# Queries and keys of two token mixers as four folded pairs with features on partitions

## The chip, the cores and the metric

The kernel runs on one core of a Trainium2 chip. The metric is the device time of one execution in microseconds (us). All arithmetic is in 32-bit floats. The engines are TensorE (PE, matmuls; its weight loads are shown apart as PEld), VectorE (DVE), ScalarE (ACT), GpSimd (POOL) and SyncE (SP, which issues nearly all transfers of weights).

## The reference

Two transformer blocks over 256 tokens of width 1024. The change lies in the first block's mixer, which runs two linear-attention branches (GLA with learned gates, retention with fixed decays) over the tokens ("latents") and takes its start states from 256 context tokens. Cut to what matters:

```python
def mixer_heads(h, w_in, gla_lr_w, gla_lr_b, gla_norm, states, rope):
    (gq, gk, gv, gg, glr_f, glr_b, rq, rk, rv, rg, m_gla, m_ret) = split_columns(h @ w_in)
    gq = heads(gq, GLA_HEADS) * GLA_DK ** -0.5          # 4 heads of 128
    gk, gv = heads(gk, GLA_HEADS), heads(gv, GLA_HEADS)
    def log_gate(lr, d):                                # lr: 16 columns a direction
        z = (lr @ gla_lr_w[d] + gla_lr_b[d]).astype(jnp.float32)
        return heads(jax.nn.log_sigmoid(z) / GLA_TAU, GLA_HEADS)
    o_f, s_gf = gla_scan(gq, gk, gv, log_gate(glr_f, 0), states[0], False)
    o_b, s_gb = gla_scan(flip(gq), flip(gk), flip(gv), flip(log_gate(glr_b, 1)), states[1], True)
    o_gla = rmsnorm(o_f + flip(o_b), gla_norm) * jax.nn.silu(heads(gg, GLA_HEADS))
    ...  # the same for retention with rq, rk, rv, rotated by axial_rope for the latents
```

It is computed once for the context (only the end states are used: keys and values) and once for the latents (queries, keys, values). gq, gk, rq, rk are 512 columns of `w_in` each. For the latents the kernel needs them with features on partitions and tokens on columns; for the context it needs the keys with tokens on partitions.

## The kernel before

**Stream and ring.** All large weights are a list of 1 MB column tiles (1024 x 256, laid out as 128 partitions x 2048). SP loads them in order into a ring of six; tile t is loaded once what read tile t - 6 is through (`FREED`, built by `plan()` beside `SUMS`, the order of all sums). `tile()` on PE waits for the landing of the next one. Besides the ring, SP loads eight tiles of another weight and the inputs at the start.

**Sums and banks.** `fresh(name)` takes PSUM banks 0 to 3 in turn and waits until the sum four places earlier was read (`sum_taken`). `feature_rows` computes one tile as 16 matmuls with weights stationary, 128 rows high, and 256 token columns moving (each matmul is two records in the trace).

**Folded pairs.** `folded` computes two column tiles (512 columns) of one or two sources as seven block products in place of eight. A block is 128 tokens x 512 of the inner dimension by 512 x 256 columns, 4 matmuls with activations stationary and 256 weight columns moving. Sources are the latents (banks 0 to 3, `hl`, `folds_l`, `parts_l`) and the context (banks 4 to 7, `hc`, `folds_c`, `parts_c`). The hand-overs are:

- DVE's `rows_fold` makes four sums of activation blocks (`rows_folded`), DVE's `weights_fold` changes the tiles in place in four steps (`weights_folded`); steps 1 and 2 wait for product 1, step 3 for product 2, step 4 for product 3.
- PE: product 2 waits for `rows_folded`, product 3 for ACT's first copy of a partial sum (`part_taken`), product 4 for its second copy and weight step 1, product 5 for step 3, product 6 for ACT's third copy, product 7 for step 4. Product 1 of the next pair waits until DVE's `blocks_summed` has made its third sum of this pair.
- ACT copies after products 1, 2 and 3; DVE sums blocks after products 4, 5, 6 and 7.

**Order around the change.** On PE, by hand: the 32 low-rank columns (`lr`); then for i = 0 to 3 two gate matmuls `z{i}0`, `z{i}1` (L1542) and one tile of `feature_rows` (L1366) out of gk0, gq0, gk1, gq1; the folded pair gkc (context only, on the two key tiles, which stay in the ring for it); folded pairs gv0, gv1 for both sources; four sums e (L1561, L1563) with the gates; rk0, rk1; rkc; rv0, rv1; rq0, rq1; eight state sums sg, sr (L1581); then the loop over eight heads with the gate tiles.

**The gates on ACT.** For each i: Abs and Relu of both z (L806, L808), Exp and Ln of both together (L810, L812), then the copy of the tile (L713). DVE adds the two parts (`la`, L2348). ACT begins block i when DVE has added block i - 1 (`la_ready`).

Of the kernel before, what the change touches and what calls it, by code (L numbers as in the profile page):

```python
# [7 lines left out]
ALU = mybir.AluOpType  # L8
# [141 lines left out]
def plan():  # L150
# [21 lines left out]
    for i, name in enumerate(("gk0", "gq0", "gk1", "gq1")):  # L172
        sums.extend([f"z{i}0", f"z{i}1"])
        tile(name)
        if name[1] == "k":
            freed[-1] = ("gkc.3",)
    folded("gkc")
    for p in range(2):
        folded(f"gv{p}")
        freed.extend([(f"gv{p}.3",)] * 2)  # L180
    sums.extend(f"e{d}{s}" for d in range(2) for s in range(2))
    for j in range(2):
        tile(f"rk{j}")
        freed[-1] = ("rkc.3",)
    folded("rkc")
    for p in range(2):
        folded(f"rv{p}")
        freed.extend([(f"rv{p}.3",)] * 2)
    for j in range(2):
        tile(f"rq{j}")  # L190
# [11 lines left out]

    def pair(name):

        folded(name)
        freed.extend([(f"{name}.3",)] * 2)
# [51 lines left out]
FOLDED_ROWS = {"gkc": 1, "gv0": 2, "gv1": 2, "rkc": 2, "rv0": 2, "rv1": 2, "mg0": 3, "mr0": 3, "mg1": 3, "mr1": 3,  # L258
# [9 lines left out]
def program(nc, stream, cdram, coldram, rowdram, biasdram, x, ctxt, cvec, wlr_d, wr_d, mem, wukv_d, out):  # L268
# [4 lines left out]
    with st:  # L273
# [217 lines left out]
        lr_ones, rows_zero = sem("lr_ones"), sem("rows_zero")  # L491
        la_ready, ctxk_ready = sem("la_ready"), sem("ctxk_ready")
# [53 lines left out]
        def turn_no(m):  # L546
            return m + (m >= 6) + (m >= 7)

# [151 lines left out]
        def _(act):  # L700
# [100 lines left out]
            for i in range(4):  # L801
                if i:
                    act.wait_ge(la_ready, 2 * i)
                for d in range(2):
                    b = take(f"z{i}{d}")
                    act.activation(spt[:, d, :], b[:, :], ACT.Abs).then_inc(act_step, 1)  # L806
                    act.wait_ge(act_step, step.one())
                    act.activation(la[:, i, d, :], b[:, :], ACT.Relu, scale=-1.0).then_inc(sum_taken, 1)  # L808
                    taken.one()
                act.activation(spt, spt, ACT.Exp, scale=-1.0).then_inc(act_step, 1)  # L810
                act.wait_ge(act_step, step.one())
                act.activation(spt, spt, ACT.Ln, bias=1.0).then_inc(act_step, 1)  # L812
                step.one()
                j = i // 2
                if i % 2 == 0:
                    copy(f"gk{j}", gk[:, 2 * j:2 * j + 2, :])
                else:
                    copy(f"gq{j}", gq[:, 2 * j:2 * j + 2, :], scale=DK ** -0.5)

            def folded(name, parts, firsts, between=None):  # L820

                at, part, _ = folded_at(name)
                act.wait_ge(sum_taken, at)
                for n in range(3):
                    if between and n:
                        between(n)
                    act.wait_ge(part_ready, part + n + 1)
                    for c, (p, first) in enumerate(zip(parts, firsts)):
                        b = bank[4 * c + (at + (2, 0, 2)[n]) % NB][:, 0:256]
                        ins = act.activation((p[:, 0, :], p[:, 1, :], first)[n], b, ACT.Copy)  # L830
                    ins.then_inc(part_taken, 1)
                for _ in range(4):
                    taken.one()

            folded("gkc", [parts_c], [gkc[:, 0, 0:256]])
# [9 lines left out]
            for j in range(2):  # L845
                copy(f"rk{j}", rqk[:, 2 * j:2 * j + 2, 1, :])
            folded("rkc", [parts_c], [rkc[:, 0, 0:256]])
# [3 lines left out]
            for j in range(2):  # L851
                copy(f"rq{j}", rqk[:, 2 * j:2 * j + 2, 0, :])
# [489 lines left out]
        def _(pe):  # L1342
# [36 lines left out]
            def folded(name, w0, w1, acts):  # L1379
# [6 lines left out]
                def product(slot, lhs, rhs, start):  # L1386
# [3 lines left out]
                    for c, source in enumerate(acts):  # L1390
                        b = bank[4 * c + (at + slot) % NB][:, 0:256]
                        for k in range(4):
                            mm = pe.matmul(b, lhs(*source, k), rhs[:, k, :], start=(start and k == 0), stop=(k == 3),  # L1393
                                           skip_group_check=True)
# [142 lines left out]
            key_tiles = []  # L1537
            for i in range(4):
                for d in range(2):
                    b = fresh(f"z{i}{d}")  # L1540
                    own = (wlr, wlr_own)[i // 2]
                    pe.matmul(b[:, :], lrT[0:65, 128 * (i % 2):128 * (i % 2) + 128], own[0:65, 512 * d:512 * d + 512],  # L1542
                              start=True, stop=True).then_inc(sum_ready, 1)
                w = tile()
                feature_rows(("gk0", "gq0", "gk1", "gq1")[i], w, hl)
                if i % 2 == 0:
                    key_tiles.append(w)
            latents, context = (hl, folds_l), (hc, folds_c)
            folded("gkc", *key_tiles, [context])
# [15 lines left out]
            key_tiles = []  # L1565
            for j in range(2):
                w = tile()
                feature_rows(f"rk{j}", w, hl)
                key_tiles.append(w)
            folded("rkc", *key_tiles, [context])  # L1570
            for p in range(2):
                folded(f"rv{p}", tile(), tile(), [latents, context])
            for j in range(2):
                feature_rows(f"rq{j}", tile(), hl)
# [617 lines left out]
        def _(dve):  # L2192
# [101 lines left out]

            def blocks_summed(name, parts, dsts, between=None):
# [15 lines left out]
                for c, (p, dst) in enumerate(zip(parts, dsts)):  # L2311
                    ins = dve.tensor_tensor(dst(0, 1), part_banks(at, c)[0], p[:, 2, :], ALU.add)
# [6 lines left out]
                for c, (p, dst) in enumerate(zip(parts, dsts)):  # L2319
                    ins = dve.tensor_tensor(dst(1, 1), p[:, 1, :], p[:, 0, :], ALU.add)  # L2320
# [5 lines left out]
                for c, (p, dst) in enumerate(zip(parts, dsts)):  # L2326
                    ins = dve.tensor_tensor(dst(1, 0), p[:, 0, :], part_banks(at, c)[3], ALU.subtract)
# [15 lines left out]
            rows_fold(hc, folds_c, ((0, 4),))  # L2343
            for n in range(8):
                i, d = divmod(n, 2)
                dve.wait_ge(sum_taken, NO[f"z{i}{d}"] + 1)
                dve.wait_ge(act_step, 4 * i + 4)
                dve.tensor_tensor(la[:, i, d, :], la[:, i, d, :], spt[:, n % 2, :], ALU.add).then_inc(la_ready, 1)  # L2348
                if n == 3:
                    rows_fold(hl, folds_l, ((0, 4),))  # L2350
            first = 5
            folded("gkc", [ring_tiles(first)[0], ring_tiles(first + 2)[0]], [parts_c], [block_of(gkc, 0)])
            for p in range(2):
                folded(f"gv{p}", ring_tiles(first + 4 + 2 * p), [parts_l, parts_c], [block_of(gv, 512 * p), block_of(gvc, 512 * p)])
# [5 lines left out]
            folded("rkc", ring_tiles(first + 8), [parts_c], [block_of(rkc, 0)])  # L2360
            dve.wait_ge(sum_taken, NO["rkc.3"] + 1)
# [7 lines left out]
            for p in range(2):  # L2369
                folded(f"rv{p}", ring_tiles(first + 10 + 2 * p), [parts_l, parts_c], [block_of(rv, 512 * p), block_of(rvc, 512 * p)])  # L2370
# [91 lines left out]
            dve.tensor_tensor(hvv[:, 0:4, :], mvv[:, 0:4, :, 0], mvv[:, 0:4, :, 0], ALU.mult).then_inc(dve_step, 1)  # L2462
            dve.wait_ge(dve_step, step.one())
            dve.tensor_tensor(hvv[:, 0:4, :], hvv[:, 0:4, :], mvv[:, 0:4, :, 1], ALU.add).then_inc(dve_step, 1)
# [844 lines left out]
```

## Time and profile before

| | |
|---|---|
| three timed runs, us | 1195.29, 1198.22, 1196.82 (median 1196.82) |
| the profiled execution: span, us (its own time goes from the first to the last instruction) | 1196.4 |
| PE busy | 1145.2 us, 96% |
| DVE busy | 493.8 us, 41% |
| ACT busy | 307.0 us, 26% |
| mean granted clock of TensorE | 0.987 of full speed |
| read from memory | 239.74 MB, mean 201 GB/s |

An engine's busy time is the union of its instructions' spans. Times in the trace count from the first instruction. The gap "idle before" of a row is the engine's idle time just before, with what released it. A share near 100% says which engine bounds the kernel over the whole; what an edit is worth is read in its own stretch.

### The profile page before, as it was taken

The page shows a single profiled execution, that of the slowest core. Times are in us where ns is not written, and L with a number is a line of the kernel's source. Part 1 is how long each engine was busy: PE and PEld are TensorE (multiplying, and loading weights), DVE is VectorE, ACT ScalarE, POOL GpSimd, SP SyncE. Part 2 cuts the span into 40 slices and gives each one's busy share as a digit, 9 for nine tenths or more (in the row PEclk, how much of TensorE's full clock was granted, in tenths as well). Part 3 has the DMA queues.
Part 4 walks back from the last instruction along what each step waited for, and adds up shares of the span by engine and source line. Part 5 has one row for each costly group of instructions (what it writes and reads, how often), then busy time and mean ns, then how long its engine had stood idle before and what let it go on. Part 6 is the DMA issues. An engine that isn't in the chain of part 4 may idle for free.

```text
span 1196.4 us, 15887 instructions
## 1 busy us (share of the span) xinstructions
PE 1145.2 (96%) x6452; PEld 844.0 (71%) x6452; DVE 493.8 (41%) x1114; ACT 307.0 (26%) x714; POOL 25.4 (2%) x43
## 2 busy tenths in 40 slices
PE   7999999999999999989999999889888989999998
PEld 6688888888877888865555554467656858887443
DVE  2324334304535676342222222328876432225555
ACT  4381010035213311141111110243484231000000
POOL 0000000000000030000000000010000000000000
PEclk9999999999999999999999999999889999999999
DMA  9933112322388445548999999623300414444540
GB/s 381 389 149 141 71 71 80 134 74 101 136 327 335 188 148 234 215 159 339 425 427 424 426 425 425 275 106 127 121 1 18 187 46 155 160 141 168 174 150 35
DMA packets 34727, 241.85 MB, mean 202 GB/s; under 512 B 3946, under 2 KB 4202, under 8 KB 6364
## 3 DMA queue, kind: packets, MB, share of 16 engines
q1 hardware_dynamic: 33500, 234.46, 49.7%
q0 software_dynamic: 720, 3.12, 0.7%
q10 hardware_dynamic: 432, 3.23, 0.6%
q8 instruction: 53, 0.87, 0.3%
q14 instruction: 22, 0.18, 0.0%
HBM read 239.74 MB, written 1.05 MB: 201 GB/s over the span
## 4 chain that ended last, share of the span: by engine, by line
PE 89%; DVE 3%; ACT 3%; DMA 2%; SPq 1%; issue 1%; DVEq 0%; ACTq 0%
PE bank L1393 20%; PE bank L1366 13%; PE bank L1783 9%; PE bank L1375 9%; PE bank L2139 8%; PE bank L1810 5%; PE bank L1441 4%; PE bank L1745 3%; PE bank L1752 2%; DMA arena<-in_stream 2%; PE bank L1461 1%; PE bank L1633 1%; PE bank L1636 1%; PE bank L1581 1%; PE bank L2118 1%; SPq L581 1%
## 5 line engine op out<-in xcount | busy, mean ns | idle before, releaser
L1393 PE MATMUL bank<-ring,arena 128*128 128x256 f32 x784 | 173.5, 380 | 0.7 <-ACT arena L1225 0.7
L1393 PEld LDWEIGHTS bank<-ring,arena 128*128 128x128 f32 x784 | 149.1, 190 | 21.1 <-ACT arena L1225 1.0
L1366 PE MATMUL bank<-arena,ring 128*128 128x256 f32 x480 | 103.8, 380 | 0.0
L1366 PEld LDWEIGHTS bank<-arena,ring 128*128 128x128 f32 x480 | 91.4, 190 | 12.2
L713 ACT ACTIVATE arena<-bank 128x512 f32<-128x512 f32 x58 | 34.1, 601 | 202.8 <-PE bank L1366 136.2
L1375 PE MATMUL bank<-ring,arena 128*128 128x256 f32 x320 | 71.1, 381 | 0.0
L1375 PEld LDWEIGHTS bank<-ring,arena 128*128 128x128 f32 x320 | 60.6, 191 | 9.1 <-issue 0.8
L1783 PE MATMUL bank<-ring,arena 128*64 128x256 f32 x512 | 57.0, 381 | 0.0
L830 ACT ACTIVATE arena<-bank 128x256 f32<-128x256 f32 x60 | 21.7, 382 | 136.9 <-PE bank L1393 136.9
L1375 PE MATMUL bank<-ring,hTl 128*128 128x256 f32 x256 | 56.6, 380 | 0.0
L1366 PE MATMUL bank<-hTl,ring 128*128 128x256 f32 x256 | 56.2, 380 | 0.0
L1366 PEld LDWEIGHTS bank<-hTl,ring 128*128 128x128 f32 x256 | 48.8, 190 | 8.6 <-issue 2.4
L1375 PEld LDWEIGHTS bank<-ring,hTl 128*128 128x128 f32 x256 | 48.4, 190 | 8.0 <-issue 1.9
L1783 PEld LDWEIGHTS bank<-ring,arena 128*64 128x64 f32 x512 | 36.0, 137 | 24.0 <-issue 6.7
L1441 PE MATMUL bank<-ring,arena 128*128 128x256 f32 x224 | 51.4, 386 | 1.7 <-ACT arena L713 0.8
L1441 PEld LDWEIGHTS bank<-ring,arena 128*128 128x128 f32 x224 | 42.6, 194 | 8.3 <-ACT arena L713 1.0
L1048 ACT ACTIVATE arena<-bank 128x256 f32<-128x256 f32 x16 | 6.1, 383 | 157.9 <-PE bank L1783 157.9
L1393 PE MATMUL bank<-ring,hTl 128*128 128x256 f32 x192 | 45.6, 381 | 0.4 <-ACT arena L713 0.4
L2694 DVE TENSOR_TENSOR arena<-arena,bank 128x256 f32<-128x256 f32 x16 | 6.7, 422 | 94.5 <-ACT arena L1048 94.5
L3159 DVE TENSOR_TENSOR arena<-arena 128x512 f32<-128x512 f32 x16 | 11.1, 692 | 75.7 <-ACT arena L713 75.7
L1393 PEld LDWEIGHTS bank<-ring,hTl 128*128 128x128 f32 x192 | 36.3, 190 | 5.8 <-issue 1.1
L2700 DVE TENSOR_TENSOR consts<-bank,arena 64x512 f32<-64x512 f32 x32 | 22.0, 688 | 38.6 <-PE bank L1810 38.4
(506 smaller groups left out, 1772.7 us busy)
## 6 DMA issues: line engine op xcount, KB each, us to landing
ring<-in_stream SPq DMA_DIRECT2D x163, 1024.0 KB, 7.0
arena<-in_stream SPq DMA_DIRECT2D x38, 1024.0 KB, 13.5
hTl<-in_stream SPq DMA_DIRECT2D x9, 1024.0 KB, 11.4
hTc<-in_stream SPq DMA_DIRECT2D x9, 1024.0 KB, 13.3
consts<-in_consts ACTq DMA_DIRECT2D x1, 3081.0 KB, 17.2
arena<-in_mem SPq DMA_DIRECT2D x2, 512.0 KB, 4.7
arena<-in_x SPq DMA_DIRECT2D x1, 1024.0 KB, 18.7
arena<-in_ctx SPq DMA_DIRECT2D x1, 1024.0 KB, 23.2
```

The costliest lines, as they stand in the source:

```text
L713: act.activation(dst, b[:, :].rearrange("p (a b) -> p a b", b=two), func, scale=scale).then_inc(sum_taken, 1)
L830: ins = act.activation((p[:, 0, :], p[:, 1, :], first)[n], b, ACT.Copy)
L1366: mm = pe.matmul(b[:, 256 * n:256 * n + 256], w[:, k, 128 * n:128 * n + 128], h[:, k, :], start=(k == 0), stop=(k == KD - 1))
L1375: mm = pe.matmul(b[:, 256 * i:256 * i + 256], h[:, k, 128 * i:128 * i + 128], w[:, k, :], start=(k == 0), stop=(k == KD - 1))
L1393: mm = pe.matmul(b, lhs(*source, k), rhs[:, k, :], start=(start and k == 0), stop=(k == 3), skip_group_check=True)
L1441: mm = pe.matmul(b[:, 256 * i:256 * i + 256], h[:, k, 128 * i:128 * i + 128], w[:, k, :], start=(k == 0 and i == 0), stop=(k == KD - 1), s ...
L1745: mm = pe.matmul(bank[1 + k % 2][:, 256 * j:256 * j + 256], xn2[:, j, 128 * k:128 * k + 128], Pm[:, j, :], start=True, stop=True)
L1752: mm = pe.matmul(acc[2 * j + n][:, :], hT_PT[j][:, 256:384], expert_rows(j, quad)[:, 512 * n:512 * n + 512], start=False, stop=False, skip ...
L1783: mm = pe.matmul(bank[0][CAP * e:CAP * e + CAP, FF * a:FF * a + FF], rows_k[:, at:at + CAP], w[e][:, k, :], start=(k == 0), stop=(k == KD ...
L1810: mm = pe.matmul(bank[1 + m][to:to + CT, :], hT_PT[n % 2][:, of:of + CT], wd[e][:, k, 512 * m:512 * m + 512], start=(k == 0), stop=(k == 1 ...
L2139: mm = pe.matmul(prod[m][:, :], lhs, rhs, start=(q == 0), stop=(q == 15))
L2700: ins = dve.tensor_tensor(expert_rows(g ^ n % 2, n // 2)[own, c], bank[1 + m][own, :], g2bc[own, c], ALU.mult)
```

## The change

1. gq, rq, gk and rk of the latents are computed as four folded pairs of column tiles. For features on partitions the roles in a matmul are exchanged: the (folded) weights are stationary, 128 columns at a time, and 128 tokens of the (folded) activations move. A product is then 8 matmuls of 128 columns. gk and rk take the context along as second source, in the old form.
2. The order becomes: z00, z01, z10, z11, gq, z20, z21, z30, z31, rq, gk with context, gv0, gv1, e, rk with context, rv0, rv1, states. The stream of tiles is put in the same order.
3. The gate matmuls go to banks 4 to 7 with semaphores of their own (`z_ready`, `z_taken`). ACT runs gates 0 before gq's copies, Abs and Relu of gates 1 between gq's second and third copy, Exp and Ln after the third; the same with gates 2 and 3 around rq.
4. DVE folds the rows of the latents first; its order is: gates 0, weight folds of gq, gates 1, row folds of the context, sums of gq, gates 2, weight folds of rq, gates 3, sums of rq, then gk.
5. The scale of gq by 128 ** -0.5 falls away, and the eps of the GLA head norm is multiplied by 128 instead; one small DVE operation is saved there.

```diff
             def folded(name, w0, w1, acts, features=False):
...
                         for k in range(4):
+                            if features and c == 0:
+                                for n in range(2):
+                                    mm = pe.matmul(b[:, 128 * n:128 * n + 128], rhs[:, k, 128 * n:128 * n + 128], lhs(*source, k),
+                                                   start=(start and k == 0 and n == 0), stop=(k == 3), skip_group_check=True)
+                            else:
+                                mm = pe.matmul(b, lhs(*source, k), rhs[:, k, :], start=(start and k == 0), stop=(k == 3),
+                                               skip_group_check=True)
...
...
@@ PE
-            key_tiles = []
+            latents, context = (hl, folds_l), (hc, folds_c)
             for i in range(4):
                 for d in range(2):
-                    b = fresh(f"z{i}{d}")
                     own = (wlr, wlr_own)[i // 2]
+                    if i >= 2:
+                        pe.wait_ge(z_taken, 2 * i + d - 3)
+                    pe.matmul(bank[4 + (2 * i + d) % 4][:, :], lrT[0:65, 128 * (i % 2):128 * (i % 2) + 128],
+                              own[0:65, 512 * d:512 * d + 512], start=True, stop=True).then_inc(z_ready, 1)
-                w = tile()
-                feature_rows(("gk0", "gq0", "gk1", "gq1")[i], w, hl)
...
-            folded("gkc", *key_tiles, [context])
+                if i % 2 == 1:
+                    folded(("gq", "rq")[i // 2], tile(), tile(), [latents], features=True)
+            pe.wait_ge(z_taken, 8)
+            folded("gk", tile(), tile(), [latents, context], features=True)
...
-            folded("rkc", *key_tiles, [context])
+            folded("rk", tile(), tile(), [latents, context], features=True)
...
-            for j in range(2):
-                feature_rows(f"rq{j}", tile(), hl)
@@ ACT
+            for i, (name, first) in enumerate((("gq", head_block(gq)(0, 0)), ("rq", head_block(rqk[:, :, 0, :])(0, 0)))):
+                gates_begun(2 * i)
+                gates_ended()
+                folded(name, [parts_l], [first], between_gates(2 * i + 1))
+                gates_ended()
+            folded("gk", [parts_l, parts_c], [head_block(gk)(0, 0), gkc[:, 0, 0:256]])
@@ DVE
-            rows_fold(hc, folds_c, ((0, 4),))
...
+            rows_fold(hl, folds_l, ((0, 4),))
...
+            for i, (name, v) in enumerate((("gq", gq), ("rq", rqk[:, :, 0, :]))):
+                gates_added(2 * i)
+                weights_fold(name, *ring_tiles(first + 2 * i))
+                gates_added(2 * i + 1)
+                if i == 0:
+                    rows_fold(hc, folds_c, ((0, 4),))
+                blocks_summed(name, [parts_l], [head_block(v)])
```

## Rows read from the trace of the kernel before

**Rows 1.** The page: busy time, DMA share in 40 slices, chain by engine.

```profile
PE 1145.2 (96%) x6452; PEld 844.0 (71%) x6452; DVE 493.8 (41%) x1114; ACT 307.0 (26%) x714; POOL 25.4 (2%) x43
...
DMA  9933112322388445548999999623300414444540
...
PE 89%; DVE 3%; ACT 3%; DMA 2%; SPq 1%; issue 1%; DVEq 0%; ACTq 0%
```

**Rows 2.** PE timeline, 56 to 92 us: start, length, engine, line, operation, tiles, count.

```profile
56.65 1.96 PE L1542 MATMUL bank<-arena 65*128 65x512 f32 x4 [0.68 <-ACT arena L799]
...
67.07 7.07 PE L1366 MATMUL bank<-hTl,ring 128*128 128x256 f32 x32
...
91.23 1.03 PE L1393 MATMUL bank<-ring,hTc 128*128 128x256 f32 x4
```

**Rows 3.** Windows: length, busy time and count by engine, granted clock, DMA share, GB/s.

```profile
91.23:103.32 12.09, 12.09 (x57) 10.66 (x56) 7.91 (x11) 1.75 (x4) 0.00 (x0) 1.00 0.00 1
103.32:127.50 24.18, 24.18 (x114) 21.33 (x113) 9.02 (x15) 1.98 (x6) 0.00 (x0) 1.00 0.43 174
156.82:170.63 13.81, 13.81 (x65) 12.19 (x64) 1.34 (x3) 1.19 (x2) 0.00 (x0) 1.00 0.12 51
```

**Rows 4.** PE timeline at 293 us; loads by line: count, busy, mean ns.

```profile
293.43 0.39 PE L1608 MATMUL bank<-arena 128*128 128x128 f32 x2
...
294.55 0.39 PE L1613 MATMUL bank<-arena 128*128 128x128 f32 x2
...
L1393 PEld LDWEIGHTS bank<-ring,arena 128*128 128x128 f32 x784 | 149.1, 190 | 21.1 <-ACT arena L1225 1.0 <-DVE arena L2265 0.4
```

**Rows 5.** ACT timeline, 57.5 to 94 us.

```profile
57.79 0.60 ACT L806 ACTIVATE arena<-bank 128x512 f32<-128x512 f32 x1 [1.39 <-PE bank L1542]
...
60.15 1.28 ACT L810 ACT_TABLE_LOAD   x1
...
63.81 1.06 ACT L812 ACTIVATE arena<-arena 128x1024 f32<-128x1024 f32 x1
...
93.22 0.38 ACT L830 ACTIVATE arena<-bank 128x256 f32<-128x256 f32 x1 [1.19 <-PE bank L1393]
```

**Rows 6.** DVE timeline, 64 to 100 us and 407.4 to 410.4 us.

```profile
64.97 1.29 DVE L2348 TENSOR_TENSOR arena<-arena 128x512 f32<-128x512 f32 x2 [8.69 <-ACT arena L812]
...
74.87 0.68 DVE L2262 TENSOR_TENSOR arena<-hTl 128x512 f32<-128x512 f32 x1
...
76.92 0.69 DVE L2265 TENSOR_TENSOR arena<-hTl,arena 128x512 f32<-128x512 f32 x1
...
93.16 1.23 DVE L2273 TENSOR_TENSOR ring<-ring 128x1024 f32<-128x1024 f32 x1 [0.96 <-PE bank L1393]
...
96.96 1.23 DVE L2280 TENSOR_TENSOR ring<-ring 128x1024 f32<-128x1024 f32 x1
...
407.46 0.42 DVE L2303 TENSOR_TENSOR arena<-bank,arena 128x256 f32<-128x256 f32 x1
...
409.11 0.43 DVE L2320 TENSOR_TENSOR arena<-arena 128x256 f32<-128x256 f32 x1
```

**Rows 7.** The ring's load issued at 28.5 us: its duration and time to landing.

```profile
L568 SPq DMA_DIRECT2D ring<-in_stream x1: 439/439/439, 28.5 to 28.5; - x1
...
DMA to landing us min/median/max: 33.8/33.8/33.8
```

**Rows 8.** PE timeline at 375 us.

```profile
375.77 0.48 PE L1393 MATMUL bank<-ring,hTl 128*128 128x256 f32 x1
```

**Rows 9.** Windows at pauses of PE and behind them, columns as in rows 3.

```profile
846.10:848.20 2.10, 0.07 (x1) 0.07 (x2) 2.07 (x5) 1.69 (x4) 0.00 (x0) 1.00 0.72 289
848.40:855.20 6.80, 6.11 (x31) 4.52 (x30) 5.09 (x28) 4.32 (x13) 0.00 (x0) 0.50 0.11 45
763.80:765.40 1.60, 0.09 (x5) 0.03 (x1) 1.38 (x2) 0.00 (x0) 0.00 (x0) 1.00 1.11 440
765.40:769.00 3.60, 3.60 (x8) 1.42 (x8) 0.00 (x0) 0.00 (x0) 0.00 (x0) 1.00 0.91 325
```

More of the change, by code:

```diff
@@ L170, in folded, with pair @@
         sums.extend(f"{name}.{n}" for n in range(4))
[L172 to L180, printed above, removed]
-    sums.extend(f"e{d}{s}" for d in range(2) for s in range(2))
-    for j in range(2):
[L183 to L190, printed above, removed]
+    def pair(name):
+        folded(name)
+        freed.extend([(f"{name}.3",)] * 2)
+    for name in ("gq", "rq", "gk", "gv0", "gv1"):
+        pair(name)
+    sums.extend(f"e{d}{s}" for d in range(2) for s in range(2))
+    for name in ("rk", "rv0", "rv1"):
+        pair(name)
     sums.extend(f"sg{h}" for h in range(HEADS))
@@ L800, in _ @@
             taken.one()
[L801 to L818, printed above, removed]
             def folded(name, parts, firsts, between=None):
@@ L829, in folded @@
                         b = bank[4 * c + (at + (2, 0, 2)[n]) % NB][:, 0:256]
+                        if n == 2 and len(first.shape) == 3:
+                            b = halves(b)
                         ins = act.activation((p[:, 0, :], p[:, 1, :], first)[n], b, ACT.Copy)
@@ L833, in folded, with gates_begun, gates_ended, between_gates @@
                     taken.one()
-            folded("gkc", [parts_c], [gkc[:, 0, 0:256]])
+            def gates_begun(i):
+                if i:
+                    act.wait_ge(la_ready, 2 * i)
+                for d in range(2):
+                    act.wait_ge(z_ready, 2 * i + d + 1)
+                    b = bank[4 + (2 * i + d) % 4]
+                    act.activation(spt[:, d, :], b[:, :], ACT.Abs).then_inc(act_step, 1)
+                    act.wait_ge(act_step, step.one())
+                    act.activation(la[:, i, d, :], b[:, :], ACT.Relu, scale=-1.0).then_inc(z_taken, 1)
+            def gates_ended():
+                act.activation(spt, spt, ACT.Exp, scale=-1.0).then_inc(act_step, 1)
+                act.wait_ge(act_step, step.one())
+                act.activation(spt, spt, ACT.Ln, bias=1.0).then_inc(act_step, 1)
+                step.one()
+            def between_gates(i):
+                def run(n):
+                    if n == 2:
+                        gates_begun(i)
+                return run
+            for i, (name, first) in enumerate((("gq", head_block(gq)(0, 0)), ("rq", head_block(rqk[:, :, 0, :])(0, 0)))):
[4 more added lines that the diff above has]
+            folded("gk", [parts_l, parts_c], [head_block(gk)(0, 0), gkc[:, 0, 0:256]])
             for p in range(2):
@@ L844, in _ @@
                     taken.one()
-            for j in range(2):
-                copy(f"rk{j}", rqk[:, 2 * j:2 * j + 2, 1, :])
-            folded("rkc", [parts_c], [rkc[:, 0, 0:256]])
+            folded("rk", [parts_l, parts_c], [head_block(rqk[:, :, 1, :])(0, 0), rkc[:, 0, 0:256]])
             for p in range(2):
@@ L2369, in _ @@
             for p in range(2):
[L2370 removed]
+                folded(f"rv{p}", ring_tiles(first + 12 + 2 * p), [parts_l, parts_c], [block_of(rv, 512 * p), block_of(rvc, 512 * p)])
             def gla_factors(h):
```

75 lines of the change are left out of this document (30 added, 45 removed).

## The prediction

> **What bounds the kernel now.** I read the page first: PE's busy line, the DMA slices and the chain [rows 1]. TensorE (PE) is busy 96% of the span and makes 89% of the chain that ended last. The other engines lie far below. So a shorter sum of PE work shortens the kernel, as long as nothing opens a gap on PE. Next I read PE's timeline of the changed stretch [rows 2] and its windows [rows 3]. From 56.65 us PE runs without a pause: two gate matmuls, then one column tile, four times over; a tile is half of the 13.81 us of [rows 3], 6.91 us, and 8.63 us is what one round takes ((91.23 - 56.65) / 4 = 8.64), so the two gate matmuls take 1.72. At 91.23 the first folded pair starts. The windows of the products are full to the last hundredth, at a granted clock of 1.00. The reader is to see that this stretch has no slack on PE and, so far, no gap either.
>
> Then I asked what the other engines do there, because the change reorders exactly their hand-overs. ScalarE (ACT) works 7.1 us on each block of gates: from 57.79 to 60.15 the four Abs and Relu, to 64.87 Exp and Ln, each behind a table load of 1.28 us [rows 5]. VectorE (DVE) waits for ACT and adds two halves in 1.29 us [rows 6]. Each block of ACT lies beside 8.63 us of PE work (1.72 + 6.91), and only one small copy per block ties PE to ACT. That is why it is hidden. The ring's loads are late as well: the DMA engines are full in the first two slices, to 60 us [rows 1].
>
> **The change part by part: PE's work.** Four pairs (gq, rq, gk, rk) are eight tiles of 6.91 us, 55.3 us by [rows 3] (13.81 for two). In their place stand 4 x 7 products of 8 matmuls that are 128 wide. The nearest rows are the six score matmuls of a head [rows 4]: each is two records, and five of them start within 1.12 us, from 293.43 to 294.55, so 0.223 each. A product takes 8 x 0.223 = 1.78 us, a pair 12.49, four pairs 50.0: 5.3 us less. Half the width does not cost exactly half (0.432 for 256 columns, since 6.91 us hold 16), for each record still loads 128 weight columns. Its load is on record with 190 ns [rows 4], and two of them are in flight at a time. The bounds of this price: 0.216, half of 0.432, gives 1.6 us less over 224 matmuls; a load that could not overlap the next one gives 0.380 a matmul, 35 us more. I take 0.223, as these rows are of the same width and type.
>
> The Trainium skill, "TensorE: Matmul & The Clock Gate", Part 3 (what overlaps and what doesn't), says that a weight load overlaps matmuls in flight only where its row group differs. All loads here have full height, so by this rule the four pairs would cost load and stream in turn, and the change would lose heavily. The trace disagrees: full-height matmuls follow each other at 0.223 us although two loads of 190 ns belong to each.
>
> The context halves of gk and rk (7 products of 4 matmuls, 12.09 us for each pair [rows 3]) stay as they are, inside the same pair. The eight gate matmuls stay too, 0.86 us each. New for DVE are four weight folds of 1.23 us for each of gq and rq, and for all four pairs the sums of the latents, 0.42 us an operation [rows 6]; ACT copies three blocks of 0.38 us a pair in place of two tiles [rows 5]. For gk and rk this lies beside 24.6 us of PE: in the two-sided value pair, with the same folds, copies and sums, DVE is busy 9.02 us of 24.18 and PE has no gap [rows 3]. For gq and rq, beside 12.5 us of PE, it must be followed hand-over by hand-over.
>
> **Where the early stretch gets its gaps.** Three things move, and on PE all later work is queued behind each wait. (a) gq now needs both its tiles before its first matmul. The second of them, tile 6, is issued at 28.5 us and lands after 33.8 us, at 62.3 [rows 7]; before, it was needed only at 67.07. PE's four gate matmuls end at 56.65 + 4 x 0.86 = 60.1, and everything on PE is queued behind the wait until 62.35: **first gap 2.25 us**. Nothing in the change alters the loads queued ahead of it. (b) PE's third and fourth products wait for ACT copies, which stand behind a whole block of gates; the fifth waits for the third weight fold, which DVE starts after adding that block. Block 0 ends on ACT at 64.87, DVE adds until 66.2, and the four folds take 5.03 us from 93.16 to 98.19 in the rows, with waits between them, so they are done at about +1.2, +2.4, +3.7 and +5.0 [rows 6]: 67.4, 68.6, 69.9, 71.2. Products one to three run 62.35 to 67.7, the fourth to 69.5, the fifth starts at 70.0, and gq ends at 70.0 + 3 x 1.78 = 75.35. (c) The sums of gq stand on DVE behind block 1 and the context fold. ACT starts block 1 after the second copy and after DVE has added block 0 (66.3), so 66.5 to 68.85, copies the first block of gq until 69.25 and ends block 1 at 74.0. DVE adds to 75.3, folds the context rows in 2.7 us to 78.0 and reaches the third sum 2.1 us later (407.46 to 409.54 in the rows), 80.1 [rows 6]. PE has done four gate matmuls to 78.8 and cannot start rq before 80.15: **second gap 1.35 us**.
>
> rq repeats it. Block 2 starts 1.14 us after its first gate matmul (57.79 against 56.65 in [rows 2, 5]), which is at 75.35, so 76.5 to 83.55. PE's third product waits for its copy (84.0), DVE adds to 84.9 and folds at 86.1, 87.3, 88.6, 89.9. The fourth product starts at 86.2, the fifth at 88.7, the pair ends at 94.05. ACT's block 3: 85.0 to 87.35, copy to 87.75, end 92.5; DVE adds to 93.8, and sums to 95.9. gk starts at 96.0: **third gap 1.95 us**. Before, the pair with the context keys starts at 91.23 [rows 2]. So this stretch, with the same four tiles, ends 4.8 us later.
>
> **What is given back.** From there on all is on PE, as in the two-sided value pairs, which have no gap [rows 3]. gk and rk cost 7 x (1.78 + 1.73) = 24.56 us each, 49.1 together. Removed are 12.09 + 13.81 + 12.09 + 13.81 = 51.8. That is 2.7 us less. The state products follow rv1 directly instead of rq; they need its banks one at a time, the last 5.2 us after the pair, and DVE's last sum takes under 1 us. SP's queue: the ring tile of the fifth gate is now released by rv1's last product instead of 6.9 us earlier, and is used only after eight state products and four gate tiles, over 40 us later. The DVE edit of the head variances removes one operation on 8 columns; PE is in the adaptive rows' matmuls meanwhile and starts its next pair at 375.77 with no idle time [rows 8], so it is worth nothing. Without that cover it would be worth at most what four such operations take, under 1 us. The removed scale of gq costs nothing either way.
>
> Sum at full clock: +4.8 - 2.7 = **+2.1 us**.
>
> **The clock.** The rows behind an idle PE are the part that tips it [rows 9]. After 2.1 idle us at 846.1 the granted clock was 0.50 for 6.8 us; two more pauses of 1.9 and 2.4 us, from 958.6 and 796.7, were followed by 0.50 as well; after a pause of 1.5 us at 763.8 it stayed 1.00. 0.50 is the lower of the engine's two levels, 1.2 GHz. The first and third gap are like those that a fall followed. The shortest falls in the trace last 3.4 us, the one of the rows 6.8, and I take 3.4: it costs 1.7 us of PE work. After the first gap 0.5 of it hides in the wait for the third weight fold, and 1.2 remain: gq ends at 76.55, all later chains follow, and the second gap becomes about 2.05. After the third gap it costs all 1.7, as gk has no slack. Sum: 2.1 + 1.2 + 1.7 = +5.0 us. The profiled execution has 1196.4 us of span, 0.4 under the median of the runs shown, so the forecast on the runs' side is 1196.8 + 5.0 = 1201.8 us.
>
> **Rivals.** (1) Gaps without falls of the clock: +2.1, 1198.9 us. For it: the stretch is at 1.00 today; against it: [rows 9]. (2) Also the second gap is followed by a fall: it delays rq's third product and so block 3, about +1.7, 1203.6 us. (3) The other side: DVE and ACT keep up, so that only PE's sum counts. The mechanism is the hand-over before gk: with gk's start at 93.9 the change is worth nothing, before 91.5 it is over 0.2% faster, and with no gap at all 5.3 us, 1191.5. Against it: ACT's four blocks and the copies between them (4 x 7.08 + 6 x 0.38) lead from 57.8 to 88.4 without any wait, with DVE's add and sums to 91.9, so a gk start before 91.5 asks for ACT blocks shorter than the rows show. (4) The new matmuls do not hold 0.223 in long runs, but wait for each load of 190 ns in turn: +35 us, 1232. The row group rule of the Trainium skill above is this case; the rows of scores speak against it.
>
> **How the numbers follow.** What a measurement of this kernel can tell from no change is about 0.2%, 2.4 us. My forecast with its falls has 0.5, rival 2 0.19, rival 1 0.24, rival 3 0.05, rival 4 0.02. Rival 1 lies at +2.1, just within 0.2%, and I leave 0.04 of it above. So slower is 0.5 + 0.19 + 0.02 + 0.04 = 0.75, within 0.2% is the other 0.20 of rival 1, and faster 0.05. The range reaches from rival 1 with part of the cheaper bound of the width, 0.5 of 1.6 us (1198.4), to rival 2 with 0.8 us for waits of DVE or ACT that last a little longer than read (1204.4).
>
> **What would show it.** In the changed trace: PE idle from about 60 to 62.3 in front of its first 128-wide matmul with the ring's DMA as releaser; gq's end near 75 to 77; idle 1 to 2 us before rq and about 2 before gk, both released by DVE; gk's start at 96 to 99; a granted clock of 0.5 in one or two short windows between 63 and 102 us; 0.223 us a matmul elsewhere; everything after rv1 merely shifted. The prediction is wrong if tile 6 lands early, if DVE's sums reach their third stage before PE is through its gate matmuls, or if the clock stays at 1.00.

## The result and the profile after

The changed kernel takes 1202.94 us (median of 14 runs, 1196.65 to 1206.99) against 1196.12 us for the kernel before (14 runs). The ratio is 1.0051, with a 95% interval of 1.0039 to 1.0063: 6.1 us slower, between 4.7 and 7.5. The prediction said 1201.8 us, 5.0 us slower. The profiled execution has a span of 1200.8 us, 4.4 us over that of before.

The page of the changed kernel, its busy line, the granted clock in slices and the chain by engine, against [rows 1]:

```profile
PE 1139.2 (95%) x6644; PEld 842.1 (70%) x6644; DVE 512.0 (43%) x1145; ACT 305.7 (25%) x718; POOL 25.5 (2%) x43
...
PEclk9999999999999999999999999989999999999999
...
PE 86%; ACT 5%; DVE 4%; DMA 2%; SPq 1%; issue 1%; DVEq 0%; ACTq 0%
```

PE is busy 6.0 us less than before, and the kernel is slower all the same. (Not all of the 6.0 us is work saved: the mean granted clock of the two executions differs too, 0.990 after and 0.987 before.) So PE has more idle time, and its share of the chain fell from 89% to 86% in favour of ACT (3% to 5%) and DVE (3% to 4%).

PE's timeline of the changed stretch, against [rows 2] (start, length, engine, line, operation, count, and idle time before with what ended it; L1399 are the 128-wide matmuls, L1402 the others of a folded pair):

```profile
57.92 3.67 PE L1552 MATMUL bank<-arena 65*128 65x512 f32 x8 [0.57 <-ACT arena L793]
63.75 2.96 PE L1399 MATMUL bank<-hTl,ring 128*128 128x128 f32 x16 [2.16 <-issue]
...
77.96 3.60 PE L1552 MATMUL bank<-arena 65*128 65x512 f32 x8
83.46 2.02 PE L1399 MATMUL bank<-hTl,ring 128*128 128x128 f32 x16 [1.90 <-DVE arena L2327]
85.32 1.95 PE L1399 MATMUL bank<-arena,ring 128*128 128x128 f32 x16
87.11 1.95 PE L1399 MATMUL bank<-hTl,ring 128*128 128x128 f32 x16
88.89 1.97 PE L1399 MATMUL bank<-arena,ring 128*128 128x128 f32 x16
91.21 3.84 PE L1399 MATMUL bank<-arena,ring 128*128 128x128 f32 x32 [0.35 <-DVE ring L2278]
...
98.47 2.02 PE L1399 MATMUL bank<-hTl,ring 128*128 128x128 f32 x16 [1.64 <-DVE arena L2327]
100.33 1.89 PE L1402 MATMUL bank<-ring,hTc 128*128 128x256 f32 x8
```

The reader is to see three gaps: 2.16 us before gq, 1.90 before rq, 1.64 before gk, and 0.35 inside rq. (The idle time of a row counts from the recorded end of the matmul before. Counted from where the next matmul would have started, which is how the prediction counts, the three are 2.39, 2.06 and 1.79 us.) Within rq the products start 1.79 us apart (85.32, 87.11, 88.89), so the new matmuls take 0.223 us each (1.79 / 8). From the first gate matmul to the first product of gk PE needs 98.47 - 57.92 = 40.55 us; before it needed 91.23 - 56.65 = 34.58 for its gates and four tiles. That is 6.0 us more.

The load of tile 6, against [rows 7], and windows as in [rows 3], one behind the first gap and one over the pair gk:

```profile
L562 SPq DMA_DIRECT2D ring<-in_stream x1: 430/430/430, 29.0 to 29.0; - x1
...
DMA to landing us min/median/max: 34.6/34.6/34.6
```

```profile
65.10:68.50 3.40, 3.40 (x20) 3.40 (x20) 2.26 (x3) 1.42 (x2) 0.00 (x0) 0.57 1.02 419
98.47:123.14 24.67, 24.66 (x168) 23.23 (x169) 8.78 (x15) 1.98 (x6) 0.00 (x0) 1.00 0.20 83
```

Tile 6 lands at 29.0 + 34.6 = 63.6, and gq starts at 63.75. The granted clock is 0.57 in the window from 65.1, the lower level in nearly all of it, after PE stood for 2.16 us. The pair gk is full: 24.67 us, against 24.56 forecast.

ACT and DVE in the same stretch, against [rows 5] and [rows 6]:

```profile
65.08 1.06 ACT L827 ACTIVATE arena<-arena 128x1024 f32<-128x1024 f32 x1
...
75.81 1.06 ACT L827 ACTIVATE arena<-arena 128x1024 f32<-128x1024 f32 x1
79.08 0.60 ACT L819 ACTIVATE arena<-bank 128x512 f32<-128x512 f32 x1 [2.22 <-PE bank L1552]
...
87.59 0.60 ACT L819 ACTIVATE arena<-bank 128x512 f32<-128x512 f32 x1
...
93.89 1.06 ACT L827 ACTIVATE arena<-arena 128x1024 f32<-128x1024 f32 x1
```

```profile
66.24 1.29 DVE L2358 TENSOR_TENSOR arena<-arena 128x512 f32<-128x512 f32 x2 [8.58 <-ACT arena L827]
...
76.96 1.29 DVE L2358 TENSOR_TENSOR arena<-arena 128x512 f32<-128x512 f32 x2 [4.50 <-ACT arena L827]
78.17 0.68 DVE L2263 TENSOR_TENSOR arena<-hTc 128x512 f32<-128x512 f32 x1
...
82.89 0.42 DVE L2327 TENSOR_TENSOR arena<-arena 128x256 f32<-128x256 f32 x1 [0.53 <-DVE arena L2322]
...
95.05 1.29 DVE L2358 TENSOR_TENSOR arena<-arena 128x512 f32<-128x512 f32 x2 [2.57 <-ACT arena L827]
...
97.90 0.42 DVE L2327 TENSOR_TENSOR arena<-arena 128x256 f32<-128x256 f32 x1
```

Ln of block 0 ends at 66.14 and DVE adds from 66.24. Ln of block 1 ends at 76.87; DVE adds from 76.96, folds the context from 78.17, and makes its third sum (L2327) from 82.89; rq starts at 83.46. Ln of block 3 ends at 94.95; DVE adds from 95.05 and makes the third sum from 97.90; gk starts at 98.47. Block 2 could begin only at 79.08, behind its gate matmuls. Both gaps stand behind ACT's gate blocks.

The balance of the profiled execution: +6.0 to the start of gk, and +1.3 that lie ahead of the change, where the first gate matmul comes at 57.92 instead of 56.65. In six of the kernels profiled below it comes at 56.5 to 56.8, so this part belongs to one execution. From the start of gk to the first state product PE needs 151.11 us (98.47 to 249.58), and before it needed 153.65 from its first pair on (91.23 to 244.88): 2.5 us less. So the state products start 4.7 us later than before, and the whole execution ends 4.4 us later.

### The profile page after: what moved, and what is told of

It is laid out like the page before. It is cut to its first block, busy times and chain, and to the rows that moved or that the text cites. A ratio compares the mean times of both kernels' runs of the same rounds, so it can differ in the third digit from the quotient of the medians.

```text
span 1200.8 us, 16320 instructions
## 1 busy us (share of the span) xinstructions
PE 1139.2 (95%) x6644; PEld 842.1 (70%) x6644; DVE 512.0 (43%) x1145; ACT 305.7 (25%) x718; POOL 25.5 (2%) x43
## 4 chain that ended last, share of the span: by engine, by line
PE 86%; ACT 5%; DVE 4%; DMA 2%; SPq 1%; issue 1%; DVEq 0%; ACTq 0%
PE bank L1402 20%; PE bank L1784 9%; PE bank L1370 9%; PE bank L1379 8%; PE bank L2140 8%; PE bank L1811 5%; PE bank L1450 4%; PE bank L1399 3%; PE bank L1746 3%; PE bank L1753 2%; DMA arena<-in_stream 2%; PE bank L1470 1%; PE bank L1634 1%; PE bank L1637 1%; PE bank L1582 1%
## 5 line engine op out<-in xcount | busy, mean ns | idle before, releaser
L1402 PE MATMUL bank<-ring,arena 128*128 128x256 f32 x784 | 174.2, 379 | 1.0 <-ACT arena L1229 0.7
L1402 PEld LDWEIGHTS bank<-ring,arena 128*128 128x128 f32 x784 | 148.1, 190 | 21.3 <-ACT arena L1229 1.0
L707 ACT ACTIVATE arena<-bank 128x512 f32<-128x512 f32 x50 | 29.4, 602 | 176.8 <-PE bank L1370 94.6
L807 ACT ACTIVATE arena<-bank 128x256 f32<-128x256 f32 x72 | 25.6, 382 | 168.5 <-PE bank L1402 165.0
L1379 PEld LDWEIGHTS bank<-ring,arena 128*128 128x128 f32 x320 | 60.3, 190 | 10.4 <-DMA ring<-in_stream 1.6
L1052 ACT ACTIVATE arena<-bank 128x256 f32<-128x256 f32 x16 | 6.1, 384 | 157.9 <-PE bank L1784 157.9
L1402 PE MATMUL bank<-ring,hTl 128*128 128x256 f32 x192 | 45.6, 380 | 0.3 <-ACT arena L707 0.3
L1402 PEld LDWEIGHTS bank<-ring,hTl 128*128 128x128 f32 x192 | 36.2, 190 | 5.8 <-issue 1.0
L2715 DVE TENSOR_TENSOR arena<-bank,arena 64x512 f32<-64x512 f32 x32 | 22.0, 689 | 38.6 <-PE bank L1811 38.3
L1746 PE MATMUL bank<-arena 128*128 128x256 f32 x128 | 35.5, 408 | 1.9 <-DVE arena L2675 1.9
```

The costliest lines, as they stand in the source:

```text
L707: act.activation(dst, b[:, :].rearrange("p (a b) -> p a b", b=two), func, scale=scale).then_inc(sum_taken, 1)
L1379: mm = pe.matmul(b[:, 256 * i:256 * i + 256], h[:, k, 128 * i:128 * i + 128], w[:, k, :], start=(k == 0), stop=(k == KD - 1))
L1746: mm = pe.matmul(bank[1 + k % 2][:, 256 * j:256 * j + 256], xn2[:, j, 128 * k:128 * k + 128], Pm[:, j, :], start=True, stop=True)
L2715: ins = dve.tensor_tensor(expert_rows(g ^ n % 2, n // 2)[own, c], bank[1 + m][own, :], g2bc[own, c], ALU.mult)
```

## The experiments

Theory A is that of the prediction: the new matmuls save their 1.33 us a pair, and the loss is made by the hand-overs around the gates, with falls of the clock behind the gaps. Theory B: the exchanged roles themselves cost the time. All ratios are to the kernel before, from runs beside it. The timeline of each kernel is that of one execution.

**Only rk and rq folded, behind the gates.** The kernel before, with these parts of the change alone:

```diff
-            for j in range(2):
-                w = tile()
-                feature_rows(f"rk{j}", w, hl)
-                key_tiles.append(w)
-            folded("rkc", *key_tiles, [context])
+            folded("rk", tile(), tile(), [latents, context], features=True)
             for p in range(2):
                 folded(f"rv{p}", tile(), tile(), [latents, context])
-            for j in range(2):
-                feature_rows(f"rq{j}", tile(), hl)
+            folded("rq", tile(), tile(), [latents], features=True)
```

> The kernel before, with only rk (with the context) and rq folded with features on partitions, both behind the gates, rq still behind rv1. Theory A (the loss is made by the hand-overs to ScalarE and VectorE around the gates; the new matmuls cost 0.223 us each): no idle time of TensorE in these pairs, each 1.33 us shorter than its two tiles, 2.7 us in all, so about 1193.5 us against 1196.2, ratio 0.998. Theory B (the exchanged roles cost time: 128-wide matmuls or their weight loads run slower in long runs than the six score matmuls): half of the loss of the changed kernel, ratio 1.002 or more, products of more than 1.9 us.

Measured: 1194.01 us, ratio 0.9985 (0.9972 to 0.9997), 1.8 us faster; the expected 0.998 lies inside. PE's timeline of rq in this kernel:

```profile
233.49 1.95 PE L1399 MATMUL bank<-hTl,ring 128*128 128x128 f32 x16
235.28 1.95 PE L1399 MATMUL bank<-arena,ring 128*128 128x128 f32 x16
...
246.00 1.25 PE L1584 MATMUL bank<-arena 128*128 128x256 f32 x5
```

rq takes 246.00 - 233.49 = 12.51 us, against 13.81 for its two tiles [rows 3], and from 150 to 262 us no row of PE shows idle time before it. Theory B falls: half of the change, placed elsewhere, is a gain. The first rows of this kernel show something else, which concerns the kernel before too:

```profile
56.74 1.96 PE L1551 MATMUL bank<-arena 65*128 65x512 f32 x4 [0.68 <-ACT arena L804]
60.39 8.86 PE L1370 MATMUL bank<-hTl,ring 128*128 128x256 f32 x32 [1.70 <-DMA ring<-in_stream]
```

Its first tile landed at 60.3 us in this execution (issued at 28.7, 31.6 to landing) where it landed at 57.5 before (28.1 and 29.4). PE stood for 1.70 us, and the group of this tile's matmuls lasts 8.86 us where it is 7.07 in [rows 2]: from 61.4 to 63.1 the granted clock is 0.50. The first pair starts at 94.97, 38.23 us after the first gate matmul, where it is 34.58 in [rows 2]. So this execution loses 3.65 us in the old order, in code that the edit does not touch, and its span of 1196.5 us is the longest of the 12.

**The context fold moved to the start.**

```diff
             rows_fold(hl, folds_l, ((0, 4),))
+            rows_fold(hc, folds_c, ((0, 4),))
...
                 gates_added(2 * i + 1)
-                if i == 0:
-                    rows_fold(hc, folds_c, ((0, 4),))
                 blocks_summed(name, [parts_l], [head_block(v)])
```

> The changed kernel, with VectorE's fold of the context rows (2.7 us) moved from ahead of the sums of gq to the idle time before the gates. Theory A1 (ScalarE's gate blocks carry the chain): the gap before rq closes, but rq's third product then waits for the copy behind gate block 2 for about 1.7 us, gk starts where it did within 0.3 us, ratio to the kernel before stays at 1.004 to 1.006 (a little less where one fall of the clock fewer follows). Theory A2 (VectorE's queue carries it): gk starts 1.5 to 2 us earlier, ratio 1.003.

Measured: 1199.86 us, ratio 1.0037 (1.0018 to 1.0055). PE's timeline:

```profile
56.64 3.67 PE L1552 MATMUL bank<-arena 65*128 65x512 f32 x8 [0.57 <-ACT arena L793]
...
80.14 1.95 PE L1399 MATMUL bank<-hTl,ring 128*128 128x128 f32 x16
81.93 1.95 PE L1399 MATMUL bank<-arena,ring 128*128 128x128 f32 x16
85.23 2.05 PE L1399 MATMUL bank<-hTl,ring 128*128 128x128 f32 x16 [1.35 <-ACT arena L807]
87.58 2.02 PE L1399 MATMUL bank<-arena,ring 128*128 128x128 f32 x16 [0.30 <-DVE ring L2274]
...
97.22 2.02 PE L1399 MATMUL bank<-hTl,ring 128*128 128x128 f32 x16 [1.64 <-DVE arena L2327]
```

And the first operation of gate block 3 on ACT:

```profile
86.34 0.60 ACT L819 ACTIVATE arena<-bank 128x512 f32<-128x512 f32 x1 [0.88 <-DVE arena L2359]
```

rq starts without a gap, and then its third product waits 1.35 us for ACT's copy, the fourth 0.30 and the fifth 0.35 us for weight folds. gk starts 97.22 - 56.64 = 40.58 us after the first gate matmul, where the changed kernel has 40.55. The loss was moved, not removed: theory A1. The reason is on ACT: block 3 waits for DVE's addition of block 2, and begins 29.70 us after the first gate matmul (86.34 - 56.64), where it begins after 29.67 in the changed kernel (87.59 - 57.92). So closing the second gap brings gk no nearer. The ratio is lower than 1.0051, with overlapping intervals; fewer falls of the clock would explain it, but this run does not settle that.

**The sums of rq ahead of adding gates 3.**

```diff
-                gates_added(2 * i + 1)
                 if i == 0:
+                    gates_added(1)
                     rows_fold(hc, folds_c, ((0, 4),))
                 blocks_summed(name, [parts_l], [head_block(v)])
+                if i == 1:
+                    gates_added(3)
```

> The changed kernel, with VectorE's sums of rq ahead of its addition of gate block 3. Theory A: the third gap (1.64 us before gk) closes, gk starts 1.6 us earlier, and a fall of the clock behind it becomes rarer: 2 to 3 us less than the changed kernel, ratio to the kernel before about 1.003. Theory B (cost in the matmuls): no change to the changed kernel, 1.005.

Measured: 1198.55 us, ratio 1.0012 (0.9995 to 1.0029), so 4.7 us less than the changed kernel by the ratios, more than the 2 to 3 that were expected; why it is more stays open. PE's timeline, and windows behind its first two gaps:

```profile
56.66 3.67 PE L1552 MATMUL bank<-arena 65*128 65x512 f32 x8 [0.57 <-ACT arena L793]
...
81.89 3.13 PE L1399 MATMUL bank<-hTl,ring 128*128 128x128 f32 x16 [1.90 <-DVE arena L2327]
...
94.31 3.74 PE L1399 MATMUL bank<-hTl,ring 128*128 128x128 f32 x32
```

```profile
62.10:65.50 3.40, 3.24 (x15) 3.27 (x16) 0.53 (x1) 2.74 (x3) 0.00 (x0) 0.50 1.01 422
82.60:86.00 3.40, 3.40 (x18) 3.40 (x18) 1.31 (x3) 2.36 (x3) 0.00 (x0) 0.50 0.17 70
```

The third gap is gone: gk's first product is the second half of the group at 94.31 and runs on from rq's last. It starts one product of 1.79 us later, at 96.10, 39.44 us after the first gate matmul. That is 1.1 us earlier than in the changed kernel and not the expected 1.6: rq took 14.2 us here (81.89 to 96.10) in place of 12.5, behind a fall of the clock. In this execution the clock fell behind the first and behind the second gap, to 0.50 both times, and the group of rq's first product lasts 3.13 us instead of 1.95. So gaps of 1.9 us can be followed by falls here as in [rows 9]; the same second gap of 1.90 us in the changed kernel was followed by none.

**Without Exp and Ln of the gates, and the control.** Both leave out Exp and Ln of the four gate blocks; each is replaced by a copy of one column:

```diff
-                act.activation(spt, spt, ACT.Exp, scale=-1.0).then_inc(act_step, 1)
+                act.activation(spt[:, 0, 0:1], spt[:, 0, 0:1], ACT.Copy).then_inc(act_step, 1)
                 act.wait_ge(act_step, step.one())
-                act.activation(spt, spt, ACT.Ln, bias=1.0).then_inc(act_step, 1)
+                act.activation(spt[:, 0, 0:1], spt[:, 0, 0:1], ACT.Copy).then_inc(act_step, 1)
```

> The changed kernel without Exp and Ln of the four gate blocks (each replaced by a copy of one column, so 4.7 us of ScalarE a block and the table loads are left out; the gates have other values). Theory A: the second and third gap vanish, the first (landing of tile 6) stays: TensorE loses 2.2 us there and gains 5.3 in four pairs, so about 3 us below the kernel before, ratio 0.997 to 0.999. Theory B: still above 1.003.

> Control: the kernel before without Exp and Ln of the four gate blocks (each replaced by a copy of one column; the gates have other values). Theory A: ScalarE's blocks are hidden there, ratio 1.000. If it is faster than 0.998, the gain of the changed kernel without Exp and Ln was not a matter of its hand-overs.

Measured: the changed kernel without them 1193.94 us, ratio 0.9981 (0.9968 to 0.9993); the kernel before without them 1.0000 (0.9987 to 1.0013). PE's timeline of the first:

```profile
56.53 3.67 PE L1552 MATMUL bank<-arena 65*128 65x512 f32 x8 [0.57 <-ACT arena L793]
61.88 2.02 PE L1399 MATMUL bank<-hTl,ring 128*128 128x128 f32 x16 [1.67 <-issue]
...
88.61 3.74 PE L1399 MATMUL bank<-hTl,ring 128*128 128x128 f32 x32
```

Only the first gap is left, 1.67 us. gk's first product, the second half of the group at 88.61, starts one product of 1.79 us later, at 90.40, 33.9 us after the first gate matmul. The clock behind it stays at 1.00. So ScalarE's Exp and Ln are free in the old order and cost 1.0051 - 0.9981, some 8 us, in the new one; 6.7 of them lie ahead of gk's start (40.55 against 33.87 us after the first gate matmul).

**The second tile awaited one product later.**

```diff
                 product(2, lambda h, f, k: h[:, k, 0:128], w0[:, 0:4, :], True).then_inc(part_ready, 1)
+                if name == "gq":
+                    pe.wait_ge(tile_loaded[6 % RING], 16 * (6 // RING + 1))
...
-                    folded(("gq", "rq")[i // 2], tile(), tile(), [latents], features=True)
+                    folded(("gq", "rq")[i // 2], tile(), tile(i == 3), [latents], features=True)
...
-                dve.wait_ge(part_ready, part + 1)
+                dve.wait_ge(part_ready, part + 1 + (name == "gq"))
```

> The changed kernel, but TensorE waits for gq's second tile (tile 6) only ahead of the second product, and VectorE starts gq's weight folds after that product. Theory C (the first gap costs only through the fall of the clock behind it, since the chain over gate block 0 ends later anyway): the gap of about 2.2 us breaks into one of 0.4 and one of about 1.2, no fall of the clock follows, gk starts 39.4 us after the first gate matmul instead of 40.6, ratio to the kernel before about 1.004. Theory D (the wait for the tile costs by itself): gk starts 1.8 us earlier or more. Theory E (the fall costs nothing there, VectorE's folds hide it): gk's start stays at 40.6.

Measured: 1201.31 us, ratio 1.0036 (1.0020 to 1.0052). PE's timeline and two windows:

```profile
56.61 3.67 PE L1555 MATMUL bank<-arena 65*128 65x512 f32 x8 [0.57 <-ACT arena L793]
60.12 1.95 PE L1400 MATMUL bank<-hTl,ring 128*128 128x128 f32 x16
62.04 2.05 PE L1400 MATMUL bank<-arena,ring 128*128 128x128 f32 x16
65.15 2.05 PE L1400 MATMUL bank<-hTl,ring 128*128 128x128 f32 x16 [1.06 <-ACT arena L807]
...
95.85 2.02 PE L1400 MATMUL bank<-hTl,ring 128*128 128x128 f32 x16 [1.64 <-DVE arena L2330]
```

```profile
60.10:70.00 9.90, 8.19 (x66) 7.47 (x65) 4.87 (x6) 8.89 (x12) 0.00 (x0) 1.00 0.97 401
80.00:96.00 16.00, 13.50 (x113) 12.99 (x114) 9.85 (x16) 11.39 (x15) 0.00 (x0) 1.00 0.18 66
```

The gap of 2.2 us is gone (the second product starts 0.13 us late, 62.04 against 60.12 + 1.79), one of 1.06 stands at the third product, and the clock stays at 1.00. gk starts 95.85 - 56.61 = 39.24 us after the first gate matmul, 1.3 less than in the changed kernel. That is near the forecast 1.2 us of the fall, and leaves nothing for the wait itself: theory C, by one trace on each side. The ratios do not tell the two kernels apart, as their intervals overlap. This trace also gives the loss of the stretch at full clock: 39.24 - 34.58 = 4.7 us, where the prediction's sum without falls had 4.8.

**The hand-overs rewoven.** On top of the last edit, and with the context fold at the start:

```diff
# ScalarE
                 gates_begun(2 * i)
-                gates_ended()
-                folded(name, [parts_l], [first], between_gates(2 * i + 1))
+                if i == 0:
+                    gates_ended()
+                folded(name, [parts_l], [first], (None, gates_between)[i])
+                gates_begun(2 * i + 1)
                 gates_ended()
# VectorE
-                gates_added(2 * i)
                 weights_fold(name, *ring_tiles(first + 2 * i))
-                gates_added(2 * i + 1)
-                if i == 0:
-                    rows_fold(hc, folds_c, ((0, 4),))
+                gates_added(2 * i)
                 blocks_summed(name, [parts_l], [head_block(v)])
+                gates_added(2 * i + 1)
```

`gates_between` runs Exp and Ln of block 2 ahead of rq's third copy.

> The changed kernel with the hand-overs rewoven: second tile of gq awaited before its second product; ScalarE makes gq's three copies ahead of gate block 1, and runs Exp and Ln of block 2 between rq's second and third copy and block 3 behind the third; VectorE folds weights ahead of adding gates, sums gq ahead of adding block 1 and rq ahead of block 3, and folds the context rows at the start. Theory A: no gap of more than 1.2 us from the first gate matmul on, gk starts about 34.5 us after it (the kernel before starts its first pair after 34.6), then 2.7 us less: 1193.4 us, ratio 0.998. Theory B (cost outside these hand-overs): above 1.0.

Measured: 1193.46 us, ratio 0.9985 (0.9971 to 0.9998), 1.8 us faster than the kernel before; the expected 0.998 lies inside. PE's timeline:

```profile
56.81 3.67 PE L1554 MATMUL bank<-arena 65*128 65x512 f32 x8 [0.57 <-ACT arena L793]
...
65.35 2.05 PE L1399 MATMUL bank<-hTl,ring 128*128 128x128 f32 x16 [1.22 <-ACT arena L807]
...
88.93 3.74 PE L1399 MATMUL bank<-hTl,ring 128*128 128x128 f32 x32
```

One gap of 1.22 us is left. gk's first product starts 1.79 us after 88.93, at 90.72, 33.9 us after the first gate matmul, 0.7 less than the kernel before needs for the same tiles. This version is faster than the changed kernel and, with an interval that ends just below 1, than the kernel before, though not by more than the smaller edit of the first experiment. It makes several edits at once, and what each of them gives was not measured apart. Exp and Ln are all there, so the order of the hand-overs made the loss, and not ACT's load by itself.

## Why the prediction was right

**PE's work.** Right. 0.223 us a matmul held over whole pairs (12.51 us against 12.49), and so rival 4 falls: the row group rule of the Trainium skill ("TensorE: Matmul & The Clock Gate", Part 3) is not what these full-height loads do.

**The first gap.** Right in place and size (2.39 us by starts against 2.25) and in its cause: the tile lands at 63.6 here and 62.3 before, and gq starts 0.15 us later. The row of PE names no releaser for it, where the prediction expected the DMA; it has to be read from the landing.

**The second and third gap.** Right in place and cause. With the fall behind the first gap the prediction had 2.05 and 1.95 us; by starts 2.06 and 1.79 were measured. gq's end lies 20.04 us after the first gate matmul (forecast 19.9), gk's start 40.55 (forecast 34.58 + 4.8 + 1.2 = 40.6). rq takes 13.2 us from its start to its end (83.46 to 96.68), and 13.2 were forecast (82.05 to 95.25); it starts 25.54 us after the first gate matmul, where the forecast had 25.4. The third gap is smaller by this and by small differences on the way, as gk's start is set by ACT and DVE and not by rq's end. The second gap adds nothing of its own to this: the moved context fold shows that gk starts no earlier without it. The prediction's chain, from the gate matmuls over blocks 2 and 3 to gk, holds that too.

**What is given back.** Right: 2.5 us by the traces, where 2.7 were forecast. Behind it the work is shifted, but not evenly: the state products start 4.7 us later than before, the matmuls of 128x64 at 537.60 us 5.2 later (542.78), the end comes 4.4 later. The edit of the head variances shows no effect: the pair of [rows 8], behind it, starts at 380.48 in place of 375.77, still 4.7 later.

**The clock.** Falls behind gaps happen, as the prediction says, but not where its sum puts them. Behind the first gap a fall stands in all three traces in which this gap is 1.9 us or longer (2.16, 2.18 and 1.93 us), and in the changed kernel it costs about the forecast 1.2 us, as the second tile's experiment shows. Behind the third gap, for which the sum holds 1.7 us, none of the three traces that have this gap (1.64 us in each) shows a fall: the granted clock is 1.00 for the next 3.4 us. Behind the second gap of 1.90 us one trace has a fall and one has none. So no run shows the term of 1.7 us at its place, and that the total still came within 1.1 us of the measured one is in part luck.

What makes the rest stays open. With one fall the changed kernel is 6.0 - 2.7 = 3.3 us over before; 6.1 were measured in the timed runs, 2.8 more. Within the kernel the time follows the mean granted clock: the slowest of the 14 runs (1206.99 and 1206.95 us) have 0.984 and 0.982, the fastest (1196.65 us) has 0.993. That further falls make the 2.8 us was not measured fall by fall, and two numbers speak against counting on it. The mean granted clock of the 14 runs is 0.9875, and that of the 35 runs of the kernel before beside the first four experiments 0.9892; the difference is worth about 2.0 us of PE work over 1200 us (an estimate), of which the fall behind the first gap takes 1.7. And falls do not cost the same everywhere. Between 760 and 980 us the execution of before had 0.94, that of after (765 to 985) 0.96, some 4.4 us of PE work apart (0.02 of 220 us), and yet the shift between them went only from 5.2 to 4.4 us. Late landings of tiles are another possible part: in the first experiment's execution one of them, with the fall behind it, cost 3.65 us in the old order. The three experiments that shorten or remove a gap came out at lower ratios (1.0037, 1.0012, 1.0036), but only the interval of 1.0012 lies clear of that of the changed kernel.

**The other rivals.** Rival 1 (gaps without falls, 1198.9 us) does not hold for the profiled execution, by the first window; of the 14 runs three (1196.65, 1196.96 and 1198.57 us) are as fast as it says. Rival 2 (a fall behind the second gap too) has a trace in the experiment with the sums of rq, with falls behind the first and the second gap: block 3 starts 30.99 us after the first gate matmul there (87.65 - 56.66), 1.3 later than in the changed kernel, where the prediction had about 1.7. No trace shows three falls in the stretch. Rival 3 (no gaps) is what the kernel without Exp and Ln comes near: without ACT's long blocks the second and third gap vanish. The moved context fold shows that DVE's fold ahead of the sums does not carry the loss; but DVE's order has a part, as the third gap goes when DVE sums rq ahead of adding gates 3.

## What to carry to other kernels

Seven block products in place of eight save PE time but add hand-overs between products; before such a change, add up the queue of each engine that stands between two products as carefully as PE's own sum, and put the pairs where these queues are short. A gap that is closed on one engine can come back at the next waits, with the same end of the stretch, when a third engine carries the chain; so measure to the next fixed point (here gk's start), and not by the gap. A gap of about 2 us on PE can cost more than itself when the clock falls behind it: splitting the first wait in two kept the clock at 1.00 and brought gk 1.3 us nearer, though nothing was taken out of the chain over the gates. And read how late tiles and falls of the clock lie in more than one execution before a difference of a few us is put down to an edit.

## What had not been expected of the hardware

- An arrival of data changes from run to run by about as much as the effects here. The same load of the ring landed at 62.3 us before and at 63.6 after, and the first tile, in time before (57.5 us), landed at 60.3 in the first experiment and made PE stand for 1.70 us. In both these executions PE's first matmuls behind the wait ran in part at the lower clock (2.96 us for a product in place of 1.95, 8.86 for a tile in place of 7.07); behind a gap of 1.67 us, in the kernel without Exp and Ln, they did not (2.02 us).
- A wait for a transfer is not always shown as one. The first gap is recorded on PE with "issue" as its end, though the tile lands at 63.6 and the matmul starts at 63.75; in the first experiment the same kind of wait is put down to the DMA.
- Within one kernel the mean granted clock of an execution varied by 0.011 and its time by 10.3 us (14 runs), more than the whole effect of the change.
